# Sampled values in 1 KB rows on alternate partitions, sampled states in 2 KB and 4 KB rows

## The reference, cut to what matters

```python
past_v = v_pool[page_table].reshape(B, -1, H_MOBA, HEAD_DIM)
...
top_s, top_i = lax.top_k(gate, K)
...
vg = vb[bi, hi, idx].astype(jnp.float32)
...
p = jax.nn.softmax(s.reshape(B, Q, H, -1), axis=-1).reshape(s.shape)
return jnp.einsum('bqhtk,bqhtkd->bqhd', p, vg)
```

```python
S = S * jnp.exp(g_t)[..., None, None]
u = b_t[..., None] * (v_t - jnp.einsum('bhde,bhd->bhe', S, k_t))
S = S + jnp.einsum('bhd,bhe->bhde', k_t, u)
```

## Time and profile before

| | |
|---|---|
| Median of 3 runs | 1586.29 us (1583.83 to 1589.07) |
| The profiled execution: its own time | 1587.01 us |
| The profiled execution: span from first to last instruction | 1585.2 us |
| PE busy | 1526.7 us (96%) |
| DVE busy | 943.6 us (60%) |
| ACT busy | 646.0 us (41%) |
| POOL busy | 186.9 us (12%) |
| Data moved | 365.16 MB, mean 230 GB/s |

### The profile page before, as it was taken

How to read it: one execution, slowest core, us unless ns; L and a number is a source line. 1 busy time by engine, 2 the same in 40 slices (tenths; PEclk the granted TensorE clock), 3 DMA queues, 4 the chain that set the end, 5 groups by cost and what they waited for, 6 DMA issues and landing times.

```text
span 1585.2 us, 36013 instructions
## 1 busy us (share of the span) xinstructions
PE 1526.7 (96%) x14584; PEld 1481.5 (93%) x14584; DVE 943.6 (60%) x1143; ACT 646.0 (41%) x757; POOL 186.9 (12%) x287
## 2 busy tenths in 40 slices
PE   7999999999999789999999999999999999999996
PEld 7999999999898679998899999999999999999995
DVE  4445746567763345774586666666666644445566
ACT  5444343334424353474543333543333333333344
POOL 0000202021877300101000000000001000000000
PEclk9999999999999999999999999999999999999998
DMA  8788878785988975756645545556677555555453
GB/s 293 277 324 332 320 284 337 282 330 205 283 255 260 269 271 203 287 184 239 213 161 186 171 175 183 183 175 215 237 251 264 205 179 177 183 185 185 159 179 115
DMA packets 105635, 365.16 MB, mean 230 GB/s; under 512 B 14529, under 2 KB 48650, under 8 KB 78634
## 3 DMA queue, kind: packets, MB, share of 16 engines
q1 hardware_dynamic: 90834, 322.66, 58.5%
q0 software_dynamic: 12896, 39.73, 7.3%
q10 hardware_dynamic: 1792, 1.20, 0.3%
HBM read 353.27 MB, written 10.47 MB: 229 GB/s over the span
## 4 chain that ended last, share of the span: by engine, by line
PE 75%; SPq 10%; DVE 6%; DMA 3%; issue 3%; ACT 3%; ACTq 0%; DVEq 0%
PE psum_g L518 21%; PE psum_g L519 21%; PE psum_g L520 21%; SPq L603 5%; PE M L2177 3%; DVE wl L502 3%; PE M L2192 3%; SPq L635 2%; ACT wh L497 1%; PE M L518 1%; PE psum_g L2481 1%; PE M L519 1%; PE M L520 1%; SPq L675 1%; DMA raw<-w_in_t 1%
## 5 line engine op out<-in xcount | busy, mean ns | idle before, releaser
L518 PE MATMUL psum_g<-xh,wh 128*128 128x264 f32 (+1 forms) x2382 | 696.2, 292 | 7.7 <-DVE wl L502 4.2
L502 DVE TENSOR_TENSOR wl<-raw,wh 128x2048 fp32r<-128x2048 f32 (+1 forms) x221 | 502.8, 2275 | 304.0 <-ACT wh L497 303.1
L519 PE MATMUL psum_g<-xl,wh 128*128 128x264 f32 (+1 forms) x2382 | 677.2, 284 | 0.0
L520 PE MATMUL psum_g<-xh,wl 128*128 128x264 f32 (+1 forms) x2382 | 676.7, 284 | 0.0
L497 ACT CAST wh<-raw 128x2048 fp32r<-128x2048 f32 (+1 forms) x221 | 414.6, 1876 | 258.8 <-PE psum_g L520 203.9
L518 PEld LDWEIGHTS psum_g<-xh,wh 128*128 128x128 f32 x2382 | 450.1, 189 | 22.2 <-issue 14.9
L519 PEld LDWEIGHTS psum_g<-xl,wh 128*128 128x128 f32 x2382 | 450.3, 189 | 3.1 <-issue 2.9
L520 PEld LDWEIGHTS psum_g<-xh,wl 128*128 128x128 f32 x2382 | 448.3, 188 | 0.0
L518 PE MATMUL psum_g<-gh,wh 128*128 128x264 f32 x704 | 200.5, 285 | 0.2 <-DVE wl L502 0.2
L520 PE MATMUL psum_g<-gh,wl 128*128 128x264 f32 x704 | 199.6, 283 | 0.0
L519 PE MATMUL psum_g<-gl,wh 128*128 128x264 f32 x704 | 199.6, 283 | 0.0
(11 more groups left out here) (443 smaller groups left out, 1743.7 us busy)
## 6 DMA issues: line engine op xcount, KB each, us to landing
raw<-w_t SPq DMA_DIRECT2D x88, 1024.0 KB, 4.8
raw<-w_in_t SPq DMA_DIRECT2D x53, 1024.0 KB, 7.8
kring<-cache_k_t SPq DMA_DIRECT2D x96, 512.0 KB, 5.0
sraw<-cache_k_t SPq DMA_DIRECT2D x32, 512.0 KB, 6.5
raw<-w_out_t SPq DMA_DIRECT2D x16, 1024.0 KB, 4.9
raw<-w2a_t SPq DMA_DIRECT2D x16, 1024.0 KB, 4.8
raw<-w2b_t SPq DMA_DIRECT2D x16, 1024.0 KB, 4.8
raw<-w2c_t SPq DMA_DIRECT2D x16, 768.0 KB, 4.2
```

The source lines that it names most:

```text
L502: eng.tensor_tensor(wl[:, u % 2, 0:nk], raw[:, u % 2, 0:nk], wh[:, u % 2, 0:nk].bitcast(F32), ALU.subtract).then_inc(raw_used, 1)
L518: nc.tensor.matmul(out, hi_w, x_hi(k), start=(k == order[0]), stop=False)
L519: nc.tensor.matmul(out, hi_w, x_lo(k), start=False, stop=False)
L520: last = nc.tensor.matmul(out, lo_w, x_hi(k), start=False, stop=(k == order[-1]))
```

## The change

The two arrays are laid out anew on the host, outside the measured time: values as page, head, row, two positions (row q holds positions q and q+64 of the page), states as sample, row, head, column.

- Values: one transfer still brings one page of one head, 64 KB, and there are as many of them, in the same order on the same queues. It now has 64 rows of 1 KB, not 128 rows of 512 B. It writes every second partition, the even ones for the first page of a block and the odd ones for the second, and in them two neighbouring places of `v_pages`.
- Scores: the gather must put each probability where its value row now lies, so it writes its two halves of 128 interleaved: a step of two elements (8 bytes) in `probs`.
- States: a half of 256 KB has 128 rows of 2 KB, not 512 rows of 512 B. The loads and stores of the feed-forward part have rows of 4 KB.

```diff
                 for t in range(6):
-                    eng.dma_start(v_pages[s][:, t], a["cache_v"][0, ds(pages[6 * n_ + t], 1), :, h].rearrange("a t d -> t (a d)"))\
-                       .then_inc(v_full[s], 16)
+                    eng.dma_start(v_pages[s][t % 2:P:2, t - t % 2:t - t % 2 + 2].rearrange("p s n -> p (s n)"),
+                                  a["cache_v_t"][ds(pages[6 * n_ + t], 1), h].rearrange("a p n -> p (a n)")).then_inc(v_full[s], 16)
...
-                        sp.dma_start(state_half(b, s), a["state_dn"][0, b, 4 * s:4 * s + 4].rearrange("h d e -> d h e"))\
+                        sp.dma_start(state_half(b, s), a["state_dn_t"][b, :, 4 * s:4 * s + 4])\
                           .then_inc(d_state[b // 4], 16)
...
-                pool.dma_start(state[:, s], a["state_dn"][0, b].rearrange("h d e -> d h e")).then_inc(h_in[s], 16)
+                pool.dma_start(state[:, s], a["state_dn_t"][b]).then_inc(h_in[s], 16)
...
-                pool.dma_start(o["dn_sample"][0, b].rearrange("h d e -> d h e"), state[:, s]).then_inc(h_out[s], 16)
+                pool.dma_start(o["dn_sample"][b], state[:, s]).then_inc(h_out[s], 16)
...
-                    block_n = sraw[0:64, 256 * n_:256 * (n_ + 1)]
+                    block_n = sraw[0:64, 256 * n_:256 * (n_ + 1)].rearrange("p (s m) -> p s m", s=2)
...
-                        dst = probs[:, 256 * j:256 * (j + 1)]
+                        dst = probs[:, 256 * j:256 * (j + 1)].rearrange("p (m s) -> p s m", s=2)
...
+    a["cache_v_t"] = np.ascontiguousarray(inputs["cache_v"][0].reshape(-1, 2, PAGE // 2, H, P).transpose(0, 3, 2, 1, 4)).reshape(
+        -1, H, PAGE // 2, 2 * P)
+    a["state_dn_t"] = np.ascontiguousarray(inputs["state_dn"][0].transpose(0, 2, 1, 3))
```

More of the change, by code:

```diff
@@ L595, in load_values @@
             _, pages = nc.values_load_multi_w_load_instructions(
-                pid_row[:, at:at + 6 * len(heads)], engines={kind}, min_val=0, max_val=a["cache_v"].shape[1] - 1,
+                pid_row[:, at:at + 6 * len(heads)], engines={kind}, min_val=0, max_val=a["cache_v_t"].shape[0] - 1,
                 skip_runtime_bounds_check_because="each value is an entry of the page table")
@@ L2583, in _ @@
             last_square(2, [xt[:, 1]])
-_PLAIN = ["cache_v", "state_dn", "state_conv", "page_table", "dn_a_log",
+_PLAIN = ["state_conv", "page_table", "dn_a_log",
           "dn_dt_bias", "dn_norm_w", "rel_bias"]
 _OUT = [("y", (P, KC, T)), ("kv", (P, 2 * H, T)), ("mem_k", (P, HX, N_MEM)), ("mem_v", (P, 2, HX * P)),
-        ("dn_prompt", (1, 1, H, P, P)), ("dn_sample", (1, NSAMP, H, P, P)),
+        ("dn_prompt", (1, 1, H, P, P)), ("dn_sample", (NSAMP, P, H, P)),
         ("edge", (P, 24, 3 + NSAMP)), ("conv_kept", (NSAMP, CONV_W - 2, 24 * P))]
@@ L2643, in returned @@
     return (y[None, :SEQ], y[SEQ:, None], kv[0][None, None, :SEQ], kv[1][None, None, :SEQ], kv[0][None, SEQ:, None],
-            kv[1][None, SEQ:, None], mem[0][None, None], mem[1][None, None], o["dn_prompt"], o["dn_sample"],
+            kv[1][None, SEQ:, None], mem[0][None, None], mem[1][None, None], o["dn_prompt"],
+            np.ascontiguousarray(o["dn_sample"].transpose(0, 2, 1, 3))[None],
             edge[None, None, :3], conv_sample[None])
```

## The result

| | before | after |
|---|---|---|
| Median, in the same session | 1586.77 us | 1603.49 us (1600.28 to 1605.97) |
| Ratio, 95% interval | | 1.0106 (1.0083 to 1.0128) |
| The profiled execution: its own time, span | 1587.01, 1585.2 us | 1600.28, 1598.4 us |

The change made the kernel 1.06% slower, 17 us. I had forecast 1575 us, 12 us faster. The profiled spans differ by 13.2 us.

What follows compares the result with a forecast made beforehand. PE was taken to wait for values, weights and states late in SP's queue. Gains of 6.5 (values), 3.4 (state waits) and 1.5 us (late weights), 11.4 in all, off 1587.0 us gave a forecast of 1575 us, range 1567 to 1585.

Steps and rivals of the forecast that it cites:

- What bounds the kernel: Before the feed-forward part's end: PE waits for values, weights and states late in SP's queue, 112.2 us for 13 groups.
- the next limit: POOL's half of the value loads: 7.96 us a group, 3 to 5.5 us behind SP's half as the next limit.
- Values on SP: SP's value loads: half of 18 us in issues longer than 0.333 us goes; SP needs 103 us, not 112.
- What PE gains from the values: PE's products with the values: of 10.9 us idle, 5 to 9 can go, 6.5 taken; POOL then limits.
- Values on POOL: POOL's value loads: 64 rows cost 0.025 us less each, 4 us over 156; lower bound nothing.
- States: State loads: 3.4 us of PE's state waits go, and half of 3.1 us behind late weights.
- The wait at `s_out`: SP, reaching states 4 to 7 sooner, newly waits for POOL's store, landing at 537 or at best 533.
- The gather: DVE's writes with a step of 8 bytes: 0 to 1.3 us on the path, taken as nothing.
- the feed-forward part: State loads and stores on POOL, beside a PE with no idle time: no gain, same length.
- D: Rival: POOL pays for rows on alternate partitions, 774 ns an issue, PE waits 28 us, 1615 us; chance 0.08 with smaller losses.
- B: Rival: number of transfers, not rows, holds SP; the 18 us stay, gain 0 to 5 us, 1582 to 1586; chance 0.26.
- The 0.06 for slower: Whole kernel: the chance given to a result slower by over 0.3%, against 0.73 for faster and 0.21 for within.

Runs made afterwards that it cites:

- e6: Kernel before plus 3 nearly empty transfers on SP in each of 13 groups of values, to delay SP: 1611.65 us, ratio 1.0172.
- e10: Changed kernel with SP's values read as 128 pieces of 512 B into the same 64 alternate partitions, two places each: 1625.48 us, ratio 1.024.
- e7: Changed kernel with one page of each later group moved from SP to POOL, a split of 11 and 13: 1612.46 us, ratio 1.0168.
- e12: Changed kernel with one of SP's two heads given to POOL in groups 5, 9 and 13: 1597.46 us, ratio 1.0072.
- e5: e1 with the 128 value rows of a page and head behind each other in HBM, still 512 B each: 1580.36 us, ratio 0.9965.
- e14: Changed kernel with SP's values back in 128 rows of 512 B, POOL's kept at 1 KB; results wrong, only time read: 1579.5 us, ratio 0.9966.
- e1: Kernel before with only the new states, values and gather as before: 1581.85 us, ratio 0.997.
- e2: Kernel before with only the new values and gather, states as before: 1607.49 us, ratio 1.0132.
- e3: Changed kernel with the 64 rows of 1 KB on adjacent partitions instead of every second one: 1599.86 us, ratio 1.0086.
- e8: e1 with the weight loads of units 39 to 44 started by ACT instead of SP: 1581.89 us, ratio 0.9974.
- e11: Changed kernel plus 12 blocks of 8 transfers of other shapes at SP's end; only issue times read, 3,244 ns with 127 rows.

## Why the prediction was wrong, by its own steps

**What bounds the kernel** was right: SP's queue, then PE. e6 and e10 move the time by moving SP's issues; e7 moves it by POOL's, the next limit that I had named. e12 takes a part of the loss back. That less time on SP than with 333 ns an issue would gain anything, no run shows: e5 and e14 shorten SP's stretch by 2 to 4 us against e1, and their times can't be told from it.

**"Values on SP" is the step that failed.** I asked what becomes of the held issues and let the issue itself stand at 0.333 us: both ends of my bound, 94 and 112 us, had that number in them. The held part shrank about as forecast. With 0.475 a group costs 12 x 0.665 + 0.94 = 8.9 us, thirteen 116, the weights 4; 120 of 126.7, so some 7 us are held where 18 were and I had said 9. But 156 issues x 0.142 = 22 us came on top: my 103 and these 22 make 125, against 126.7 measured. That these held issues shrank is not the relief that I had in mind either. In e14, with POOL's rows wide and SP's issue short, 14 of 108.5 us are held, and PE gains nothing. In the changed kernel SP offers less work (DMA share 0.69 to 0.79), so it is held less; e6, with the rows of before, shows the same, a dose of 26 us in a stretch that grew by 20.5.

**"What PE gains from the values"**, -6.5 us, came out at +20.8 (e2). It rested on that step.

**Values on POOL**: -0.025 us each from the slope over 128 and 1,024 rows; measured +0.012 (549 ns). e3 shows the slope's sign right and less than half its size, 11 ns, and the step of two partitions on top, 24 ns.

**States**: -3.4 and -1.5 us; e1 gives -4.8. Of the mechanisms, the issue of a state fell from 508 to 432 ns at the median and SP's time for states and one unit of weights from 16.6 to 9.3 in e1. The wait at `s_out` stayed away since SP came there later, not sooner; in e12 it came.

**The gather** cost nothing, 2.57 against 2.56 us; the feed-forward part kept its length: the end of unit 47 came 13.4 us later, the span 13.2.

**The rivals.** D had the right mechanism, an issuer that pays for the shape, and the right form of price, but I put it on POOL because POOL's rows showed two other shapes. For SP I had rows of one piece and of 512 and drew no rival from them. The same sum there, 13 groups x 12 x 0.142 = 22 us less the 11 of held issues, gives a slower kernel. B was right in part: the length of the rows is worth 3% of engine time and no time of the kernel (e14); but the held issues did not stay, and under B the time was to be 1582 to 1586. The 0.06 for slower was too low for an operation of which I had no row on the engine that sets the pace.

**What stays open**: why 64 partitions are slow, and 32 on every fourth; and what exactly holds an issue for over 1 us, on SP and in e8 on ACT, while the DMA engines are some 0.9 busy. The one odd shape that a page explains is 127 rows at 3,244 ns: by the Trainium skill (DMA: Bandwidth & Descriptors, Why a DMA increments its semaphore by 16 and not by 1) a transfer runs on the largest number of DMA engines, 16 at most, that divides the size of its slowest dimension, so on one for 127 rows and on 16 for 64. The trace of e11 agrees for 127 (7.1% of 16 engines); by this rule 64 would be as good as 128. On 128 partitions 128, 256 and 512 pieces take 432, 469 and 507 ns, so the number of pieces counts for little; the 596 ns of 64 pieces are not of that kind.

## What to carry to other kernels

When an engine's queue sets the pace, the time that an issue holds it is a term of the sum by itself: before a transfer changes its shape, measure that shape's issue on that queue, alone, and don't carry over the time of the old one. Fewer and longer rows are no gain as such; here 64 partitions cost 0.14 us an issue more than 128, some 22 us in all, and 1 KB rows gave nothing back over 512 B. Of this change keep the states: e1 and e5 are 0.3% faster than the kernel before (e5: 0.9965, 0.995 to 0.998).

## What the runs showed of the hardware that I had not expected

- Started by SP with fixed addresses, one behind another, a transfer holds SP for 432 ns on 128 partitions, 596 on 64, 607 on 64 in two pieces each and 617 in four, 420 on 16 and 421 on 32. On 127 it is 298 for the first and then 3,244, a wait for the transfers ahead.
- A part of the time goes with the transfer ahead: the same 1 MB of weights held SP for 0.42 us behind a value on 128 partitions and 0.58 behind one on 64.
- In the kernel, with page numbers in registers, the same step is 333 to 475 ns, and 605 for 64x2 pieces.
- POOL doesn't share it: at the median 524 ns for 64 adjacent partitions, 548 for alternate ones, 535 for 128.
- Between two groups of transfers POOL stands idle for 3.04 us when it reads 13 page numbers into registers, and for 0.91 us when it reads 12.
- A transfer of 128 rows of 32 B from HBM to HBM held SP for 590 ns, longer than a page of values.
